# Latent attention two heads at a time, rotary halves of 64 rows, and a half exchange by transfers

## The reference

```python
def mla_mixer(h, w_in, q_norm, kv_norm, w_uq, w_ukv, w_o):
    c_q, c_kv, k_rope = jnp.split(h @ w_in, [512, 1024], axis=-1)
    c_q, c_kv = rms_norm(c_q, q_norm), rms_norm(c_kv, kv_norm)
    q = (c_q @ w_uq).reshape(B, T, 16, 128 + 64)
    q_nope, q_rope = jnp.split(q, [128], axis=-1)
    kv = (c_kv @ w_ukv).reshape(B, T, 16, 128 + 128)
    k_nope, v = jnp.split(kv, [128], axis=-1)
    q_rope, k_rope = apply_rope(q_rope, cos, sin), apply_rope(k_rope, cos, sin)   # one k_rope for all heads
    scores = (q_nope @ k_nope + q_rope @ k_rope) * 192 ** -0.5
    mask = k_chunk[None, :] <= q_chunk[:, None]      # 16 meta tokens, then chunks of 64
    return softmax(where(mask, scores, -1e30)) @ v, then @ w_o

# second block, per layer, mixers 0 and 2 of four (8 heads of 64 each):
q, k = apply_rope_2(head_rms_norm(q, g), cos, sin), apply_rope_2(head_rms_norm(k, g), cos, sin)
def apply_rope_2(t, cos, sin):
    t1, t2 = t[..., :32], t[..., 32:]
    return concatenate([t1 * cos - t2 * sin, t2 * cos + t1 * sin], axis=-1)
```

## Time and profile before

| | |
|---|---|
| median of 3 runs | 3235.5 us (3234.89 to 3237.42) |
| profiled execution | 3238.18 us, its span 3236.4 us |
| PE busy | 3192.8 us, 99% |
| DVE busy | 1901.4 us, 59% |
| ACT busy | 1614.9 us, 50% |
| granted tensor engine clock, mean over the span | 0.998 |

### The profile page before, as it was taken

How to read it: one execution, slowest core, us unless ns; L and a number is a source line. 1 busy time by engine, 2 the same in 40 slices (tenths; PEclk the granted TensorE clock), 3 DMA queues, 4 the chain that set the end, 5 groups by cost and what they waited for, 6 DMA issues and landing times.

```text
span 3236.4 us, 61711 instructions
## 1 busy us (share of the span) xinstructions
PE 3192.8 (99%) x26230; PEld 3156.4 (98%) x26230; DVE 1901.4 (59%) x2149; ACT 1614.9 (50%) x2107; POOL 0.2 (0%) x4
## 2 busy tenths in 40 slices
PE   7999999999999999999999999999999999999999
PEld 7999999999999999999999999998999999999999
DVE  5765555544555467765554455556667665666664
ACT  6554534333443466754443344446556655656663
POOL 0000000000000000000000000000000000000000
PEclk9999999999999999999999999999999999999999
DMA  6235555655556555455565555654555556555554
GB/s 195 86 117 159 176 174 175 196 163 168 172 178 195 157 181 175 155 193 188 185 211 181 167 187 189 205 159 145 168 158 162 165 157 173 153 170 157 161 154 142
DMA packets 532126, 546.29 MB, mean 169 GB/s; under 512 B 8336, under 2 KB 530832, under 8 KB 530832
## 3 DMA queue, kind: packets, MB, share of 16 engines
q1 hardware_dynamic: 531984, 544.21, 53.8%
HBM read 542.08 MB, written 2.10 MB: 168 GB/s over the span
## 4 chain that ended last, share of the span: by engine, by line
PE 93%; DVE 3%; ACT 2%; issue 1%; DMA 0%; SPq 0%; DVEq 0%; ACTq 0%
PE ps L558 86%; PE ps L646 1%; PE ps L637 1%; PE ps L665 1%; PE ps L666 1%; PE ps L832 1%; PE ps L815 0%; PE ps L824 0%; DVE w_lo L1389 0%; DVE w_lo L1392 0%; PE ps L741 0%; DMA raw<-mla_w_in_dram 0%; PE ps L796 0%; PE ps L679 0%; ACT w_hi L931 0%
## 5 line engine op out<-in xcount | busy, mean ns | idle before, releaser
L558 PE MATMUL ps<-x_hi,w_hi 128*128 128x256 f32 (+1 forms) x6032 | 1708.9, 283 | 23.3 <-DVE w_lo L1515 10.2
L558 PE MATMUL ps<-x_lo,w_hi 128*128 128x256 f32 (+1 forms) x6032 | 1707.2, 283 | 0.0
L558 PE MATMUL ps<-x_hi,w_lo 128*128 128x256 f32 (+1 forms) x6032 | 1702.4, 282 | 0.0
L558 PEld LDWEIGHTS ps<-x_hi,w_hi 128*128 128x128 f32 x6032 | 1138.4, 189 | 32.5 <-issue 21.3
L558 PEld LDWEIGHTS ps<-x_lo,w_hi 128*128 128x128 f32 x6032 | 1136.4, 188 | 1.1
L558 PEld LDWEIGHTS ps<-x_hi,w_lo 128*128 128x128 f32 x6032 | 1136.9, 188 | 0.0
L1392 DVE TENSOR_TENSOR w_lo<-raw,w_hi 128x1024 fp32r<-128x1024 f32 (+2 forms) x504 | 652.7, 1295 | 589.4 <-ACT w_hi L931 589.0
L931 ACT ACTIVATE w_hi<-raw 128x1024 fp32r<-128x1024 f32 (+2 forms) x504 | 562.7, 1116 | 739.6 <-PE ps L558 721.9
L1389 DVE TENSOR_TENSOR w_lo<-raw,w_hi 128x1024 fp32r<-128x1024 f32 (+1 forms) x504 | 597.1, 1185 | 477.0 <-ACT w_hi L928 471.4
L928 ACT ACTIVATE w_hi<-raw 128x1024 fp32r<-128x1024 f32 (+1 forms) x504 | 516.1, 1024 | 431.3 <-PE ps L558 414.8
L558 PE MATMUL ps<-hid_hi,w_lo 128*128 128x272 f32 (+1 forms) x1408 | 401.0, 285 | 0.0
(11 more groups left out here) (297 smaller groups left out, 2229.2 us busy)
## 6 DMA issues: line engine op xcount, KB each, us to landing
raw<-ffn_w_gu_dram SPq DMA_DIRECT2D x176, 1024.0 KB, 5.0
raw<-w_in_dram SPq DMA_DIRECT2D x128, 1024.0 KB, 5.5
raw<-ffn_w_down_dram SPq DMA_DIRECT2D x64, 1408.0 KB, 6.6
raw<-w_out_dram SPq DMA_DIRECT2D x32, 1024.0 KB, 5.5
raw<-lru_w_in_dram SPq DMA_DIRECT2D x24, 1024.0 KB, 5.6
raw<-mla_w_o_dram SPq DMA_DIRECT2D x16, 1024.0 KB, 5.7
raw<-lru_w_o_dram SPq DMA_DIRECT2D x16, 1024.0 KB, 5.7
raw<-lru_y_gates_dram SPq DMA_DIRECT2D x8, 1280.0 KB, 5.7
```

The lines of the kernel that those rows point to most:

```text
L558: mm = pe.matmul(out, l, r, start=first and k == 0 and i == 0, stop=last and k == kn - 1 and i == 2)
```

## The change

Latent attention takes two heads per step (`pair_step`, eight pairs). A query slot holds both heads' columns (4 row blocks of 384), reordered as it is rounded (`pieces`): both heads' 128 plain columns, then one tile with the 64 rotary columns of each. So a pair has three query tiles, one rotation at line `swap`, and rotary queries and keys with one head in each half of the partitions; the input projection's rotary key columns are rounded twice into a slot, one copy for each half. A key/value slot holds 4 row blocks of 512. The rotary scores are products over 64 rows, `qr[64x:64x+64]` with `kr[64x:64x+64]`, for the two heads in turn. The first query tile sees 80 keys, the second 208, the third 272. Banks are used otherwise (plain queries and values in 2 and 3, rotary queries, transposed probabilities and results in 0 and 1, keys in 1 and 4, scores in 4 to 7). In the second block the matmuls with `swap_r`, their rounding and their difference go; SP copies `qk` to `t2` with the halves of 32 rows exchanged, in four transfers, and the vector engine multiplies `t2` by the sine. SP's loop over units is written out.

```diff
-QT = ((0, 0, 128), (80, 0, 256), (144, 64, 272))
-AB = 384
+PAIRS = HEADS // 2
+UQ = 2 * QK
+QT = ((0, 0, 80), (80, 128, 208), (144, 384, 272))
+MS = 656
...
+        def pieces(n, width, half):
+            a = first_part(width)
+            w = slice(0, a) if half == 0 else slice(a, width)
+            r, hi, lo = raw[:, n % RAW, w], w_hi[:, n % 2, w], w_lo[:, n % 2, w]
+            if n == HEAD.n - 1:
+                k = KD // 2
+                r = raw[:, n % RAW, half * k * ROPE:(half + 1) * k * ROPE].rearrange("p (k c) -> p k c", k=k)
+                pair = [t.rearrange("p (k a c) -> p k a c", k=k, a=2) for t in (hi, lo)]
+                return [(r.unsqueeze(2).broadcast_to([P, k, 2, ROPE]), *pair)]
+            if width != 4 * UQ:
+                return [(r, hi, lo)]
+            heads = r.rearrange("p (k a c) -> p k a c", k=2, a=2)
+            hi, lo = (t.rearrange("p (k c) -> p k c", k=2) for t in (hi, lo))
+            def joint(t, c):
+                return t[:, :, c].rearrange("p k (a c) -> p k a c", a=2)
+            nope, rope = slice(0, 2 * NOPE), slice(2 * NOPE, UQ)
+            return [(heads[:, :, :, 0:NOPE], joint(hi, nope), joint(lo, nope)),
+                    (heads[:, :, :, NOPE:QK], joint(hi, rope), joint(lo, rope))]
...
+                    if u > 0 and part == 0 and i == 2 and unit_kind(u - 1)[2]:
+                        swap_halves(layer, u - 1)
+            def swap_halves(layer, u):
+                sp.wait_ge(y2_made, before(u, ROTATED) + 1 + PER_LAYER[ROTATED] * layer)
+                for a in range(4):
+                    sp.dma_start(t2[32 * a:32 * a + 32, :, :],
+                                 qk[32 * (a ^ 1):32 * (a ^ 1) + 32, :, :]).then_inc(halves_swapped, 16)
...
+            def project(hs, r, begins=False):
+                n = HEAD.n + 2 * hs
+                w = slot_view(w_hi, n % 2, 4, UQ), slot_view(w_lo, n % 2, 4, UQ)
+                if begins:
+                    pe.wait_ge(pair_free[1], HEAD.p[1])
+                else:
+                    pe.wait_ge(vv_out, hs + 2 * r)
+                pe.wait_ge(lo_half, n + 1 + 4 * r)
+                three_passes(bank(2), w, cq, 0, (0, 1), True, False)
+                pe.wait_ge(lo_made, n + 1 + 4 * r)
+                three_passes(bank(2), w, cq, 0, (2, 3), False, True).then_inc(q_done, 1)
+                three_passes(bank(3), w, cq, P, (0, 1, 2, 3), True, True).then_inc(q_done, 1)
+                if begins:
+                    pe.wait_ge(pair_free[0], HEAD.p[0])
+                else:
+                    pe.wait_ge(mo_ready, 2 * hs - 1 + 4 * r)
+                three_passes(bank(0), w, cq, 2 * P, (0, 1), True, False).then_inc(slot_half, 1)
+                three_passes(bank(0), w, cq, 2 * P, (2, 3), False, True).then_inc(slot_done, 1)
+                n = n + 1
+                w = slot_view(w_hi, n % 2, 4, 512), slot_view(w_lo, n % 2, 4, 512)
...
+                pe.wait_ge(lo_half, n + 1 + 4 * r)
+                three_passes(bank(1), w, ck, 0, (0, 1), True, False)
+                pe.wait_ge(lo_made, n + 1 + 4 * r)
+                three_passes(bank(1), w, ck, 0, (2, 3), False, True).then_inc(k_done, 1)
                 pe.wait_ge(qr_out, hs + 1 + 2 * r)
-                pe.matmul(bank(1), swap, qr_raw[:], start=True, stop=True).then_inc(q_rot, 1)
+                pe.matmul(bank(0), swap, qr_raw[:], start=True, stop=True).then_inc(q_rot, 1)
+                if not begins:
+                    pe.wait_ge(ms_masked, hs + 2 * r)
+                three_passes(bank(4), w, ck, 2 * P, (0, 1, 2, 3), True, True).then_inc(k_done, 1)
+                pe.wait_ge(qn_out, 2 * hs + 2 + 4 * r)
+                three_passes(bank(2), w, ck, P, (0, 1, 2, 3), True, True).then_inc(v_done, 1)
+                three_passes(bank(3), w, ck, 3 * P, (0, 1), True, False).then_inc(slot_half, 1)
+                three_passes(bank(3), w, ck, 3 * P, (2, 3), False, True).then_inc(slot_done, 1)
...
+                def rope(x, i, start):
+                    q0, _, keys = QT[i]
+                    rows = slice(ROPE * x, ROPE * x + ROPE)
+                    return pe.matmul(out(x, i), qr[rows, q0:q0 + P], kr[rows, 0:keys], start=start, stop=not start)
+                for x in range(2):
+                    nope(x, 0, True)
+                    nope(x, 2, True)
+                for i in (0, 2, 1):
+                    for x in range(2):
+                        rope(x, i, i == 1)
+                for x in range(2):
+                    mm = nope(x, 1, False)
...
+            def pair_step(hs, r, ends=False):
                 project(hs, r)
+                pe.wait_ge(qr_made, hs + 1 + 2 * r)
+                pe.wait_ge(vt_out, 2 * hs + 1 + 4 * r)
+                turn_probs(hs - 1, r, (0, 1), 2)
                 scores(hs, r)
+                if ends:
+                    values(hs - 1, r, (0, 1))
                 turn_values(hs, r)
-                values(hs - 1, r)
+                if not ends:
+                    values(hs - 1, r, (0, 1))
...
+            def last_pair(k):
+                if k == KD - 5:
+                    values(PAIRS - 1, 0, (5, 7))
+                if k == KD - 2:
+                    pe.wait_ge(mo_ready, HEADS)
                 if k == KD - 1:
                     pe.wait_ge(mo_ready, HEADS + 1)
+            def turn_last():
+                pe.wait_ge(ms_masked, PAIRS)
+                turn_probs(PAIRS - 1, 0, (4, 6), 5)
+            pe.wait_ge(mo_ready, HEADS - 1)
+            pe.wait_ge(vv_out, PAIRS)
+            turns(WO, 4, 8, xh, xl, T, last_pair, {1: turn_last})
...
+            def pair_step(hs, r, widths=(4 * UQ, W8)):
+                for x in range(2):
+                    act.wait_ge(q_done, 2 * hs + x + 1 + 4 * r)
+                    act.activation(qn[:, x, :], ps[:, 2 + x, 0:T], ACT.Copy).then_inc(qn_out, 1)
                 hi(HEAD.n + 2 * hs + 2, r, widths[0], widths[0] == W8)
...
+                hi(HEAD.n + 2 * hs + 3, r, widths[1])
+                if widths[0] == W8:
+                    pair_result(hs - 1, r)
+                    values_out(hs, r)
+                else:
+                    values_out(hs, r)
+                    if hs > 0:
+                        pair_result(hs - 1, r)
                 exps(hs, r)
...
+                if hs > 0:
+                    pair_result(hs - 1, r)
                 dve.wait_ge(ms_exp, hs + 1 + 2 * r)
...
                     lo(n + 7, rl, W8)
                     if rotated:
-                        dve.wait_ge(y2_hi, 1 + rd)
-                        dve.tensor_tensor(head_hl[:, 1, :, :], qk[:], head_hl[:, 0, :, :].bitcast(F32),
-                                          ALU.subtract).then_inc(y2_split, 1)
-                    lo(n + 8, rl, W8)
-                    if rotated:
-                        dve.wait_ge(rot2_made, 1 + rd)
-                        dve.tensor_tensor(t2[:], ps[:, 6:8, :].rearrange("p b (a t) -> p (b a) t", a=2),
-                                          sin4, ALU.mult).then_inc(t2_made, 1)
+                        dve.wait_ge(halves_swapped, 64 * (1 + rd))
+                        dve.tensor_tensor(t2[:], t2[:], sin4, ALU.mult).then_inc(t2_made, 1)
                         dve.wait_ge(t2_made, 2 + 2 * rd)
                         dve.tensor_tensor(qk[:], t1[:], t2[:], ALU.add).then_inc(qk_made, 1)
+                    lo(n + 8, rl, W8)
```

More of the change, by code:

```diff
@@ L359, in build @@
         HEAD = Place(9, 3, 2)
[L360 removed]
+        WO = after(HEAD, PAIRS, 2, 0)
         FT = FH // 256
@@ new lines, in scores, with out, nope @@
+            def scores(hs, r, begins=False):
+                if begins:
+                    pe.wait_ge(kr_made, 1)
+                    pe.wait_ge(qr_made, 1)
+                pe.wait_ge(kn_out, 2 * hs + 2 + 4 * r)
+                def out(x, i):
+                    return (ps[:, 4 + 2 * x, 0:80], ps[:, 4 + 2 * x, 128:336], ps[:, 5 + 2 * x, 0:T])[i]
+                def nope(x, i, start):
+                    q0, _, keys = QT[i]
+                    return pe.matmul(out(x, i), qn[:, x, q0:q0 + P], kn[:, x, 0:keys], start=start, stop=not start)
+                def rope(x, i, start):
+                    q0, _, keys = QT[i]
+                    rows = slice(ROPE * x, ROPE * x + ROPE)
[8 more added lines that the diff above has]
+                    mm = nope(x, 1, False)
@@ L691, in head_step @@
-            def head_step(hs, r):
+                for x in range(2):
+                    for i, (q0, at_key, keys) in enumerate(QT):
+                        n_q = QT[1][0] if i == 0 else P
+                        for kt in range(-(-keys // P)):
+                            n = 16 if kt == 2 else P
+                            out = (ps[0:n, banks[x], q0:q0 + n_q], ps[0:n, banks[x], T + q0 - 80:T + q0 - 80 + n_q],
+                                   ps[0:n, tail, 256 + P * x:384 + P * x])[kt]
+                            mm = pe.transpose(out, ms[0:n_q, x, at_key + P * kt:at_key + P * kt + n],
```

(11 more changed lines are left out.)

331 lines of the change are left out of this document (145 added, 186 removed).

## The result

The changed kernel takes 3202.78 us (median of 4 runs, 3202.56 to 3205.52) against 3235.43 (4 runs, 3234.89 to 3237.42): a ratio of 0.990, 95% interval 0.9888 to 0.9912, 32.7 us faster. The forecast was 3202, its range 3194 to 3212. The profiled execution took 3202.56 us with a span of 3200.8.

What follows compares the result with a forecast made beforehand. Matmuls on the tensor engine were taken to bound the kernel. Less tensor work in eight pairs (-26.7 us), added waits (+4.4) and the half exchange (-11.3) gave -33.6 from 3235.5: 3202 us, range 3194 to 3212.

Steps and rivals of the forecast that it cites:

- What bounds: Whole kernel: matmuls keep the tensor engine busy 99% of the span, so a removed matmul should come off nearly whole.
- Part 1: Joint rotary tile in the pair loop: 12 matmuls fewer, 1.50 us, and one rotation fewer, 0.46 us, per pair.
- Part 2: Scores of a pair: fewer keys and overlapping 64-row rotary products, 4.46 us to 3.08, 1.38 less (bounds 0.66 and 1.61).
- Part 3: Pair loop and its ends: waits add 4.4 us, with the rotary copy as tightest point (bounds 0 and about +11).
- Part 4: Second block's rotation: transfers replace matmuls and their waits, 11.3 us less; exchange takes 4 us, hidden, 7.0 allowed in unit 0.
- First: Rotary scores: 64-row halves don't overlap in this order, +0.72 us a pair, +5.8, 3208 us; chance 0.08.
- Second: Pair loop bound by the vector and scalar engines' chain to the rotary copy: 1 us late per pair, +7, 3209; chance 0.12.
- Third: Second block: exchange queues behind a load, 9.2 us, and is late in four units, twice: +12.8, 3215 us; chance 0.07.
- The slower side: Second block: exchange late enough to eat the 33.6 us from about 11.8 us, over 0.2% slower from 12.6; chance 0.03.

Runs made afterwards that it cites:

- ends: Changed kernel with rotary keys moved ahead of the first slot's difference and the last pair's previous result between mask and maxima: 3199.91 us.
- small_tile: Changed kernel with the first query tile of the scores seeing 128 keys in place of 80: 3204.89 us, a pair 18.65 us.
- exchange_behind: Changed kernel with the four exchange transfers issued behind the next unit's fourth load, not behind its third: 3262.51 us, ratio 1.0083.
- full_height: Changed kernel with rotary keys kept per head, zeros in the other head's 64 rows, and rotary products over all 128 rows: 3207.61 us.
- two_trips: Changed kernel with first and third tiles' rotary products ahead of their plain ones, so two trips into 64-row halves per pair: 3205.1 us.
- serial_halves: Changed kernel with head one's three rotary products made before head two's, in place of alternating heads: 3202.93 us.
- full_keys: Changed kernel with 128, 256 and 272 keys per query tile as before the change, the added ones masked: 3207.3 us.
- vector_later: Changed kernel with two memsets of unused tiles on the vector engine ahead of each pair's rotary copy: 3210.25 us.

## Why the prediction was right

**What bounds.** Right. 32.5 of the span's 35.6 us are busy time that went (some 1.4 of it by the clock), the rest waits: 3.2 at the second block's rotation, the others level within 0.2.

**Part 1, query tile and rotation.** Right. 48 matmuls in 6.07 us and 36 in 4.50 cost the same per matmul as before, a rotation 0.46, and one of each is gone from a pair.

**Part 2, scores.** The mechanism was right, the sizes too kind. 3.08 us were forecast, 3.50 measured. The rotary products were 1.18 and are 1.23. The plain ones were priced at 1.90 by columns and take 2.26: 0.20 of it is the return from the halves, and 0.19 is the first tile, two products of 80 columns priced at 0.136 us each that take 0.23; the other tiles were 0.03 under their price. One price a column had been taken from a whole head's scores; the single starts within them would have shown that 128 columns cost 1.8 ns each and 272 cost 1.65. The pair's saving is 2.93 and not 3.34 us, eight times: 23.4 in place of 26.7.

The Trainium skill's page TensorEngine Tiling (Array Packing) bears on both halves of this. Its Theoretical Speedup, up to two for two 64-row tiles, is met if the 0.20 us that a second trip adds to the rotary products is the way in and is taken off: 1.23-0.20 = 1.03 us against 2.07 at full height. Its Key Properties say that changing the mode drains the array; the runs agree, with 0.20 us on either side, 0.4 of the 1.04 us that the halves would save a pair without it (2.07 less 1.03).

**Part 3, waits.** The step that failed most. +4.4 us were forecast, and the list gives: rotary keys +1.2, first key slot -2.2, first pair's value copies +0.8, rotary copy 0, last pair's result +1.6, last head's scores -0.8, in sum +0.6. The start was mis-sized because two waits there share one cause and trade with each other, as ends shows. The inner pairs wait for nothing, forecast 0.13 us each: the rotary copy's time was forecast to 0.1 us, and the scores' extra 0.42 us gave it cover. With scores as short as forecast the weight load would have wanted the copy at about T+11.5 and had it 0.3 us late in each inner pair (an estimate from these rows); the prediction had counted to the matmul. The over-priced waits (3.8) and the over-priced gain (3.3) cancel, which is why 22.3 us forecast for the first block and its attention meet 22.7 measured in the profiled executions. By the medians the pairs are worth only 20.0 to 20.2, 2 us under the forecast, and the exchange 0.7 over it. The closeness of the total is in part luck.

**Part 4, exchange.** Right in size (11.3 forecast, 11.9 to 12 measured) and in its cover (4 us forecast from normed tiles to use, 4.3 measured, 7.0 allowed). The split of the 4.3 was not forecast: SP starts to issue the last of the four 1.9 us after the first, and it lands 2.4 us later.

**Rivals.** First (no overlap, 3208): out as the main story, though neighbours in the same half are not the whole of it. Second (vector chain binds, 3209): out for this kernel by 0.1 us, in as soon as 0.4 us of vector work is added (small_tile). Third (queued behind a load): out, since the third load was issued at 2204.2, 9 us ahead of the exchange, and such a load takes 5.4; its price of 9.2 us was right when the exchange was put behind the fourth. The slower side was real as well: exchange_behind is 28 us slower than before, at 13.3 us from the normed tiles, above the 12.6 from which that was forecast. By the waits alone it would have been some 10 slower (43 less the 32.7 gained); the rest is the clock, which the prediction left out.

## What to carry to other kernels

Price small matmuls one by one, by start-to-start distances of their own width: fewer columns can buy nothing (here a full-precision product of 80 takes as long as one of 128), and what they buy on the engines that read the result is a separate sum. Count each trip into 64-row halves, here 0.4 us, and put as many products as can be into one trip. Measure the room of a copy that feeds a matmul up to the start of the weight load, not of the matmul. Where the tensor engine is made to wait for several us, count the clock behind the wait too. A transfer within the chip that replaces matmuls is cheap (4.3 us of delay, hidden) while no load stands ahead of it on its queue, and ruinous (13.3 us, of which 4.3 are the later issue) behind one.

## What was not expected of the hardware

- A trip into the 64-row halves costs 0.20 us on the plain products behind it (full_height, two_trips) and 0.20 on the rotary ones in it, which I take for the way in (two_trips).
- Three full-precision products behind one another in the same 64-row half take 1.52-0.20 = 1.32 us for two heads, 1.18 ns a column, where full height takes 1.85: a half is cheaper even without its neighbour, but for the one place where the heads change. Why is open.
- A full-precision product with 80 moving columns takes as long as one with 128 (0.23 us).
- Four transfers of 128 KB from one set of rows to another take SP 0.6 us each to issue and land 2.4 us later; behind a 1 MB load they land 6.5 us after their issue (the median of 32).
- Behind the wait near 1350 the granted clock is 0.84 over ten us in the changed kernel and 1.00 in serial_halves and ends, 1.6 us that their edits were not meant to make; the two profiles of the changed kernel both lose it. Behind each of the eight waits of exchange_behind it is 0.66 or 0.83.
- The rotation takes 0.72 us in the chain, not 0.46, when its weight load has to wait for the copy and is no longer hidden behind the matmuls before (small_tile, full_keys, vector_later).
